# A two-block transformer layer in one kernel: the second expert stage regrouped by weight rows, with a class of 32 tokens in four column tiles

## The reference

```python
logits = (xt @ router_w + router_b).astype(jnp.float32)
top_v, top_e = lax.top_k(logits, TOP_K)            # 4 of 32
gate = jax.nn.softmax(top_v, axis=-1)
def expert_block(args):
    rows, e = args
    xb = xt[rows]
    hb = xb @ w1[e] + b1[e]                        # w1[e]: 1024 x 2048
    g, u = hb[:, :D_EXPERT], hb[:, D_EXPERT:]
    g = jnp.minimum(g, SWIGLU_LIMIT)
    u = jnp.clip(u, -SWIGLU_LIMIT, SWIGLU_LIMIT)
    glu = g * jax.nn.sigmoid(g * SWIGLU_ALPHA)
    return ((u + 1.0) * glu) @ w2[e] + b2[e]       # w2[e]: 1024 x 1024
```

## Time and profile before

| what | us |
| --- | --- |
| three timed runs, median | 2508.3 |
| lowest and highest of them | 2503.12, 2519.26 |
| the profiled execution | 2512.87 |
| its span in the trace | 2511.1 |
| second expert stage in it, first up product to last down product | 1145.33 |

### The profile page before, as it was taken

One profiled execution on the slowest core, in us unless ns is written; L12 is line 12 of the kernel. 1 busy time (PEld: TensorE's weight loads), 2 busy tenths in 40 slices (PEclk: granted clock), 3 DMA queues, 4 the chain that ended last, 5 costly groups with the idle time before them and its releaser, 6 DMA issues.

```text
span 2511.1 us, 32392 instructions
## 1 busy us (share of the span) xinstructions
PE 2247.6 (90%) x12228; PEld 1328.1 (53%) x12229; DVE 589.5 (23%) x1216; ACT 370.2 (15%) x718; POOL 6.5 (0%) x23
## 2 busy tenths in 40 slices
PE   7969877889998997788858999899999999999996
PEld 5655445556545686633335554445455555555553
DVE  2352512211222015500031212111221222222113
ACT  1032101121111014300011111101011111111111
POOL 1000000000000000000000000000000000000000
PEclk9989997999999976588877989999998999999998
DMA  8822253998966340022225999859799999999990
GB/s 289 317 101 82 86 201 120 327 356 312 325 224 233 102 150 19 1 100 100 100 78 198 393 363 345 312 202 380 270 386 381 339 393 376 393 383 393 384 370 18
DMA packets 272763, 621.67 MB, mean 248 GB/s; under 512 B 12200, under 2 KB 19026, under 8 KB 272510
## 3 DMA queue, kind: packets, MB, share of 16 engines
q1 hardware_dynamic: 272302, 616.95, 67.1%
q10 hardware_dynamic: 208, 0.67, 0.1%
HBM read 616.55 MB, written 1.05 MB: 246 GB/s over the span
## 4 chain that ended last, share of the span: by engine, by line
PE 87%; DVE 6%; issue 4%; ACT 3%; POOL 0%; ACTq 0%; DVEq 0%; POOLq 0%
PE pair L1616 26%; PE pair L1410 16%; PE pair L1652 10%; PE pair L1671 8%; PE pair L1397 6%; PE pair L1689 4%; PE pair L1621 3%; PE pair L1655 2%; PE pair L1459 2%; PE pair L1451 1%; PE pair L1825 1%; PE pair L1434 1%; PE pair L1422 1%; PE pair L1702 1%; PE pair L1414 1%
## 5 line engine op out<-in xcount | busy, mean ns | idle before, releaser
L1616 PE MATMUL pair<-ring,r_at 128*64 128x256 f32 (+1 forms) x4864 | 662.0, 402 | 53.2 <-issue 49.5
L1616 PEld LDWEIGHTS pair<-ring,r_at 128*64 128x64 f32 (+1 forms) x4864 | 385.6, 143 | 317.2 <-issue 177.2
L1652 PE MATMUL pair<-ring,r_big 128*64 128x512 f32 x1152 | 263.9, 609 | 0.0
L1410 PE MATMUL pair<-ring,x_T 128*128 128x512 f32 (+1 forms) x608 | 236.9, 545 | 2.5 <-ACT r_big L719 1.1
L1671 PE MATMUL pair<-r_big,r_mix 128*128 128x64 f32 (+1 forms) x1600 | 204.3, 290 | 23.1 <-DVE r_big L1338 11.4
L1671 PEld LDWEIGHTS pair<-r_big,r_mix 128*128 128x128 f32 x1600 | 197.8, 205 | 34.0 <-issue 33.2
L1173 DVE TENSOR_SCALAR r_big<-iota,rank 128x128 f32<-128x128 f32 x100 | 24.1, 283 | 752.0 <-PE pair L1621 577.0
L1410 PEld LDWEIGHTS pair<-ring,x_T 128*128 128x128 f32 x608 | 107.5, 190 | 125.0 <-issue 123.0
L1652 PEld LDWEIGHTS pair<-ring,r_big 128*64 128x64 f32 x1152 | 80.4, 140 | 151.2 <-issue 149.9
L1397 PE MATMUL pair<-x_T,ring 128*128 128x256 f32 x656 | 152.8, 391 | 7.8 <-DVEq L838 6.4
L1397 PEld LDWEIGHTS pair<-x_T,ring 128*128 128x128 f32 x656 | 125.9, 195 | 32.3 <-issue 8.0
(11 more groups left out here) (310 smaller groups left out, 1602.7 us busy)
## 6 DMA issues: line engine op xcount, KB each, us to landing
ring<-exp_w SPq DMA_DIRECT2D x192, 2048.0 KB, 12.5
ring<-w_in SPq DMA_DIRECT2D x24, 2048.0 KB, 9.2
ring<-w_gate SPq DMA_DIRECT2D x16, 2048.0 KB, 11.4
ring<-w_up SPq DMA_DIRECT2D x16, 2048.0 KB, 13.4
ring<-w_down SPq DMA_DIRECT2D x16, 2048.0 KB, 9.2
ring<-mod_w SPq DMA_DIRECT2D x12, 2048.0 KB, 13.5
ring<-w_out SPq DMA_DIRECT2D x4, 2048.0 KB, 8.0
ring<-w_branch SPq DMA_DIRECT2D x3, 2048.0 KB, 7.6
```

Source lines behind the costliest of these rows:

```text
L1410: ins = mm(out[:, t, 0:n], xT[:, k, P * t:P * t + P], w[:, k, c0:c0 + n], start=(k == 0), stop=(k == nk - 1 and bias is None))
L1616: ins = mm(out, stat(k), w_[:, k, c0:c0 + n], start=(k == 0), stop=(bias is None and k == KD - 1))
L1652: ins = mm(ps[2][H2 * h:H2 * h + H2, 0:512], hT[:, at:at + H2], cols, start=beg, stop=end)
```

## The change

- The loads of an expert are now four of 256 whole rows of w1 (8 KB each) and two of w2 as before. All four quarters of the hidden columns are built up side by side over the four loads (`up`), in `ps[0]` (and `ps[1]`).
- A fourth class: up to 32 tokens. There each product fills 32 columns of the array, and the four quarters of the columns go to four column tiles. In down, the four parts of the contraction go to the four tiles; they are summed by the scatter, for which the slots' numbers are repeated four times (`slots_of`). With 64 slots the same is done with two.
- Gather and scatter are always made for 128 slots (`gather2`, `scatter2`), with no choice by size; the class of all 256 tokens adds its outputs in `outputs_of_all` and scatters zeros.
- The hidden rows are formed once an expert and turned at once; the scatter stands after up, then the next gather, then turn and down.
- The size is chosen twice in an expert (`up` and `down`), with nested `If`/`Else` from the smallest.
- The first expert stage gets functions of its own (`gather1`, `scatter1` and so on) with the same work as before.
- Ahead of the stage, three copies write `slots_of`, and `ranks` has two more vector instructions for 32 experts.

The core of the diff:

```diff
+        def smallest_first(eng, size, body):
+
+            with eng.If(size == 0):
+                body(H4)
+            with eng.Else():
+                with eng.If(size == 1):
+                    body(H2)
+                with eng.Else():
+                    with eng.If(size == 2):
+                        body(P)
+                    with eng.Else():
+                        body(T)
...
-            def expert2(slot, kind, e, half, wait):
+            def expert2(slot, part, e, wait):
                 sp.wait_ge(PD, wait)
-                if kind < 2:
-                    src = w1e[bass.ds(e * D, D), 1024 * kind + 512 * half:1024 * kind + 512 * half + 512]
-                    nk = KD
+                if part < 4:
+                    src, nk = w1e[bass.ds(e * D + 2 * P * part, 2 * P), :], 2
                 else:
-                    src = w2e[bass.ds(e * D + 512 * half, 512), :]
-                    nk = 4
+                    src, nk = w2e[bass.ds(e * D + 512 * (part - 4), 512), :], 4
...
+            def hidden_T2(e, w):
+
+                act.wait_ge(sem("hidden_turned2"), e + 1)
+                n = min(8 * w, 1024)
+                ins = s.copy(HTF[:, 0:n], ps[0][:, 0:n])
+                if w == T:
+                    ins = s.copy(HTF[:, 1024:2048], ps[1])
+                ins.then_inc(sem("hiddenT_ready2"), 1)
...
+                n = 512 if b == 1 and w == H2 else 1024
+                if b == 1 or w != T:
+                    act.wait_ge(PD, pd_down)
+                    s.copy(YS[:, 0:n], ps[2][:, 0:n]).then_inc(sem(f"ys_ready{b}"), 1)
...
+            rows_of(2, 0)(P)
             with looped(act, 0, NE2) as e:
-                size, size_next = size_of(act, e), size_of(act, e + 1)
+                size = size_of(act, e)
 
                 def body(w):
-                    for half in range(2):
-                        act.wait_ge(sem("gate_limited"), 2 * e + (1 + half))
-                        if half:
-                            act.wait_ge(sem("hidden_ready2"), 2 * e + 1)
-                        s.activation(SG[:, 0:4 * w], GS[:, 0:4 * w], ACT.Sigmoid, scale=1.702)\
-                            .then_inc(sem("sig_ready"), 1)
-                    turned(2, 0, e, w)
-                    by_size(act, size_next, rows_of(2, e + 1))
-                    turned(2, 1, e, w)
+                    rows, n = (H2, 512) if w == H4 else (P, 512) if w == H2 else (P, 1024)
+                    if w == T:
+                        act.wait_ge(sem("up_times_gate"), e + 1)
+                        ins = s.activation(GSG, GSG, ACT.Sigmoid, scale=1.702)
+                    else:
+                        act.wait_ge(sem("gate_limited"), e + 1)
+                        ins = s.activation(SG[0:rows, 0:n], GS[0:rows, 0:n], ACT.Sigmoid, scale=1.702)
+                    ins.then_inc(sem("sig_ready"), 1)
+                    rows_of(2, e + 1)(P)
+                    hidden_T2(e, w)
                     outputs_and_picks(2, e, w, 6 * e + (base_pd2 + 6))
 
-                by_size(act, size, body)
+                smallest_first(act, size, body)
...
+                slots = iota if b == 1 else slots_of[:, bass.ds(size_of(dve, e) * P, P)]
                 for t in range(NT):
-                    ins = v.tensor_scalar(pick[:, buf, t], iota, rank[:, t, bass.ds(e, 1)], None, ALU.is_equal)
+                    ins = v.tensor_scalar(pick[:, buf, t], slots, rank[:, t, bass.ds(e, 1)], None, ALU.is_equal)
...
+            for c, w in enumerate((H4, H2)):
+                link(v.tensor_copy(slots_of[:, P * c:P * c + P].rearrange("p (q s) -> p q s", s=w),
+                                   iota[:, 0:w].unsqueeze(1).broadcast_to([P, P // w, w])))
+            link(v.tensor_copy(slots_of[:, 2 * P:4 * P].rearrange("p (q s) -> p q s", s=P),
+                               iota.unsqueeze(1).broadcast_to([P, 2, P])))
...
+            def hidden2(e, w):
+
+                dve.wait_ge(PD, 6 * e + (base_pd2 + 4))
+                if w == T:
+                    for t in range(NT):
+                        ins = v.tensor_scalar(GSG[:, 1024 * t:1024 * t + 1024], ps[2 * t], 7.0, None, ALU.min)
+                    ins.then_inc(sem("gate_limited"), 1)
+                    for t in range(NT):
+                        ins = v.tensor_scalar(HID[:, t], ps[2 * t + 1], 7.0, -7.0, ALU.min, ALU.max)
+                    gate, up, sig, out = GSG, HIDF, GSG, HIDF
+                else:
+                    rows, n = (H2, 512) if w == H4 else (P, 512) if w == H2 else (P, 1024)
+                    gate, up, sig, out = [x[0:rows, 0:n] for x in (GS, US, SG, HIDF)]
+                    g_in, u_in = {H4: (ps[0][0:H2, 0:512], ps[0][H2:P, 0:512]), H2: (ps[0][:, 0:512], ps[0][:, 512:1024]),
+                                  P: (ps[0], ps[1])}[w]
+                    v.tensor_scalar(gate, g_in, 7.0, None, ALU.min).then_inc(sem("gate_limited"), 1)
+                    ins = v.tensor_scalar(up, u_in, 7.0, -7.0, ALU.min, ALU.max)
+                ins.then_inc(up_free, 1)
+                dve.wait_ge(sem("gate_limited"), e + 1)
+                dve.wait_ge(up_free, e + 1)
+                v.scalar_tensor_tensor(out=up, in0=up, scalar=1.0, in1=gate, op0=ALU.add, op1=ALU.mult)\
+                    .then_inc(sem("up_times_gate"), 1)
+                dve.wait_ge(sem("up_times_gate"), e + 1)
+                dve.wait_ge(sem("sig_ready"), e + 1)
+                v.tensor_tensor(out=out, in0=up, in1=sig, op=ALU.mult).then_inc(sem("hidden_ready2"), 1)
+
+            def outputs_of_all(e):
+
+                dve.wait_ge(PD, 6 * e + (base_pd2 + 6))
+                for t in range(NT):
+                    for h in range(2):
+                        v.scalar_tensor_tensor(out=ACC[:, t, 512 * h:512 * h + 512], in0=ps[2 + t][:, 512 * h:512 * h + 512],
+                                               scalar=comb0[:, t, bass.ds(e + 1, 1)],
+                                               in1=ACC[:, t, 512 * h:512 * h + 512], op0=ALU.mult, op1=ALU.add)
+                v.memset(YS, 0.0).then_inc(sem("ys_ready2"), 1)
...
+                        hidden2(e, w)
+                        dve.wait_ge(sem("hidden_ready2"), e + 1)
                         add_outputs(2, e, ACC)
-                        hidden2(e, 1, w)
-
-                    by_size(dve, size_of(dve, e), body)
-                    dve.wait_ge(sem("hidden_ready2"), 2 * e + 2)
+                        if w == T:
+                            dve.wait_ge(sem("outputs_added2"), e + 2)
+                            outputs_of_all(e)
+
+                    smallest_first(dve, size_of(dve, e), body)
+                    dve.wait_ge(sem("outputs_added2"), e + 2)
+                    dve.wait_ge(sem("ys_ready2"), e + 2)
...
+            def up_parts(w):
+
+                x32, x64, x128 = [lambda k, n=n: XG[:, k, 0:n] for n in (H4, H2, P)]
+                if w == H4:
+                    return [(ps[0][H4 * q:H4 * q + H4, 0:512], x32, q, H4) for q in range(4)]
+                if w == H2:
+                    return [(ps[0][H2 * (q % 2):H2 * (q % 2) + H2, 512 * (q // 2):512 * (q // 2) + 512], x64, q, H2)
+                            for q in range(4)]
+                if w == P:
+                    return [(ps[q // 2][:, 512 * (q % 2):512 * (q % 2) + 512], x128, q, P) for q in range(4)]
+                return [(ps[2 * t + q // 2][:, 512 * (q % 2):512 * (q % 2) + 512],
+                         lambda k, t=t: XT[:, k, P * t:P * t + P], q, P) for t in range(NT) for q in range(4)]
+
+            def up(j, i, size, e, buf):
+
+                def body(w):
+                    if w >= P:
+                        pe.wait_ge(sem("pickT_ready2"), e + 1)
+                    if w == T:
+                        pe.wait_ge(sem("ys_ready2"), e + 1)
+                        pe.wait_ge(sem("outputs_added2"), e + 1)
+                    for n in range(4):
+                        pe.wait_ge(slot_loaded[(j + n) % RING], value_of(j + n, i, 6))
+                        w_ = ring[:, ((j + n) % RING) * SLOT:((j + n) % RING + 1) * SLOT]\
+                            .rearrange("p (t n) -> p t n", t=2)
+                        for k in range(2 * n, 2 * n + 2):
+                            for out, stat, q, rows in up_parts(w):
+                                ins = mm(out, stat(k), w_[:, k % 2, 512 * q:512 * q + 512], start=(k == 0), stop=False)
+                        if n == 3:
+                            for out, stat, q, rows in up_parts(w):
+                                ins = mm(out, ones[32 * q:32 * q + 1, 0:rows], b1q[32 * q:32 * q + 1, buf], start=False,
+                                         stop=True)
+                        ins.then_inc(PD, 1)
+                    if w >= P:
+                        pe.wait_ge(up_free, e + 1)
+
+                smallest_first(pe, size, body)
...
+            def down(j, i, size, e):
+
+                def body(w):
+                    if w == H4:
+                        for c in range(4):
```

(62 more changed lines are left out.)

190 lines of the change are left out of this document (75 added, 115 removed).

## The result

The changed kernel takes 2538.7 us (median of 4, 2527.3 to 2549.0) against 2505.7 us of the kernel before on the same chip (median of 4, 2501.2 to 2519.3): ratio 1.0121, interval 1.0062 to 1.0181. It is slower by 1.2%, where 2430 was forecast. The profiled execution is the 2527.3 us one.

What follows compares the result with a forecast made beforehand. TensorE and the loads were both taken as near their limits. With loads as pace, 939 + 4 + 47 + 34 + 36 = 1060 us of stage against 1145.3; 2512.9 - 85.3 + 2 = 2430 us, range 2395 to 2455 (0.48).

Steps and rivals of the forecast that it cites:

- I add 3 us for a lower clock (below) and jumps: 24: TensorE's small expert (at most 32 tokens): 20.9 us of work plus 3 us for clock and jumps, 24 us.
- about 1.5 for the jump over the smaller class's body: Experts of 33 to 64 tokens: TensorE's jump, covered by no queued work, takes about 1.5 us.
- debt: TensorE's lag behind the loads: each large expert inside the stage falls 31 us behind; a small one pays off 6 us.
- C: Rival: TensorE waiting for loads lowers its clock in small experts, 28 to 30 us each; 2480 to 2510 us; chance 0.11.
- Four column tiles: Small class's up and down: four tiles four times as fast as full width; up 6.9 us, bias 1.05, down 3.45.
- Rival A: Four column tiles run only two at a time: up 13.8 us, down 7; 2562 us, slower; chance 0.09.
- Rows of 8 KB: Loads of the first weight go at 419 GB/s, 5.0 us each against 5.45; an expert's six take 30.3 us.
- Rival B: The 8 KB rows bring nothing (385 GB/s): 32.1 us of loads an expert; 2465 us; chance 0.19.
- The new wait behind the turn: Small experts: TensorE stands about 1.2 us before down while ScalarE copies the gathered, then the turned rows.
- Large experts: Over 64 tokens (4 experts): 61 us each against 54, with new waits for picks (1.3 us) and PSUM (2.6 us).
- Class of 33 to 64: Six experts: column work of up and down as before, full scatter, jump added; 34 us each against 30.6.
- The sum: Second expert stage, loads as pace plus debts: 1060 us against 1145.3, giving 2430 us.

Runs made afterwards that it cites:

- e10: Changed kernel with TensorE's second expert stage held twice, without and with the 256-token class, chosen once ahead of the loop: 2431.8 us, ratio to before 0.9683.
- e11: Changed kernel with the 256-token body replaced by dead products, another number at each of the four places of a pass: 2481.0 us (one run).
- e7: e2 without the 32-token class, so that small experts go by the 64-token class: 2494.1 us, ratio 0.993.
- e12: e2 with w1 read in 2 KB pieces, two loads of 1 MB for a slot: 2466.3 us, ratio 0.9815.
- e2: Changed kernel without TensorE's 256-token code in up and down of the second stage: 2430.1 us, ratio 0.9669.
- e1: Changed kernel with the size chosen for each load (four up slots, the turn, each down half), so no jump exceeds 12.3 KB: 2507.0 us, ratio 0.9997.
- e6: e2 with the 256-token code for four experts put back as one never-taken branch at each pass's end: 2466.1 us, ratio 0.9811.
- e9: Changed kernel with the 256-token class kept as an expert of its own, chosen once at the expert's start: 2593.6 us, ratio 1.0325.

## Why the prediction was wrong

**The step that failed** is the jumps' part of "I add 3 us for a lower clock (below) and jumps: 24", with the "about 1.5 for the jump over the smaller class's body" beside it. Jumps were counted by how many there are ("two size choices an expert instead of some eleven"), as a thing of which fewer is better. The runs show that what counts is how much code a jump passes, with a step at some 20 KB: both jumps reach it here, none of the eleven did. A small expert pays 2.7 to 4.1 us behind bias and 1.5 to 2.8 us more in scatter, whose granted clock has fallen after the stand, and ten of the 22 pay another 1.8 to 3.5 us behind down. With short jumps (e10) a small expert that waits for nothing takes 20.8 us, as the sum before those 3 us had it (20.9); in the changed kernel one without a wait for loads, inside a pass, takes 28.4 to 31.6. That is the pace of the loads, and so the second half of the error: no small expert pays off anything of the debt a large one leaves, on which the sum's 1060 us rested.

No rival named it. C had a part of the consequence (the clock takes it back) with another cause, the wait for loads; over the changed kernel's stage the granted clock is 0.89, where C wanted under 0.75, and in e10, which waits for loads more, it is 0.92 and the gain stands. The prediction's own sign of being wrong (small experts more than 33 us apart or less than 28) missed it: they stand 31.6 us apart.
The Trainium skill (Runtime: NRT & Kernel Launch, Instruction fetch mechanics) has the mechanism: instructions are fetched ahead in sequence, in blocks of 16 KiB, and a taken branch out of a window of two blocks stops the engine until its target is fetched. The traces agree: packets of 16 KB, one landing in or just before each stand, no stand at 18.4 KB in most cases, one in every small expert at 37 KB. With two blocks a jump of between one and two block lengths is free or not by where in its block it starts. That fits the 20.0 KB behind down, which stand at two places of the pass and not at the other two; it doesn't explain the five values at 18.4 KB in e11, which all lie at the same place, so the moment matters too. Neither was tried by itself. The same section also gives TensorE 128 KiB; with a window of that size the jumps of 18 to 37 KB should have cost nothing, and the measurement decides against it.

**Four column tiles**: up x64 in 7.07 us (forecast 6.9), bias 0.99 (1.05), down 3.64 (3.45). Rival A falls. The tiles are worth 64 us (e7).

**Rows of 8 KB**: 417 to 425 GB/s (419). Rival B falls, and its price was right: 35 us forecast for no gain from the rows, 36 measured (e12 against e2).

**The new wait behind the turn**: 1.2 us forecast, 34.0 us in 28 waits measured (L1776 above), 1.2 each.

**Large experts**: 61, measured 61.2 and 58.7 in e10. The first is partly luck: the three take 63.9, 60.3 and 59.3 us, and the 63.9 hold one stand of 6.2 us behind the wait for PSUM, which ends 1.55 us after an instruction packet has landed. Of its terms, the wait for the up rows to leave PSUM is there as said (2.6 forecast), here the last expert of the changed kernel:

```profile
2473.49 1.23 DVE r_big L1380
2474.72 1.14 DVE r_big L1381
...
2476.38 5.37 PE pair L1837 x8
```

**Class of 33 to 64**: 34 forecast; 37.8 measured, 34.1 in e10. The jump over 27.6 KB behind up accounts for 1.3 us of the 3.7 (stands of 1.5 to 2.5 us in four of six); in two of the six up takes 20.5 us, not 16.7, one of them with a stand of 2.36 us inside it that ends 1.4 us after a packet has landed. The rest stays open.

**The sum**: with the long jumps gone (e10) the stage from first up product to last down product is 1058.6 us, where 1060 was forecast (1165.0 in the changed kernel), and the time 2431.8, where 2430 was. Most terms hold one by one, so this is not luck alone. That it comes out within 2 us is luck, since some of them cancel: the 3 us for clock and jumps aren't needed by a small expert that waits for nothing, a large one takes 58.7, not 61; small experts follow each other in 28.2 us in the mean, under the 30.3 of the loads, because behind a large one they run at TensorE's pace, and debts and waits at pass starts take more than their share (stands of up to 9.3 us ahead of up).

**Why e1 gained little** is settled only in part. Its packets (160) show that short jumps pass code that is fetched, and each of its experts has some 76 KB of it, five packets in 31.7 us for a small one. Stands inside up and behind bias say that in a burst of four slots TensorE outruns the fetch: 21 of the 26 stands over 1.5 us inside or ahead of up end 1.4 to 1.8 us after a packet has landed. The packets around the chain shown start at 1362.8, 1369.4, 1375.4, 1381.2 and 1387.6 us. Of the 159 distances over the stage 102 are 5.5 to 6.5 us and eight are shorter. Five of them take nearly as long as the whole expert, so the fetch may well be e1's pace. No run varies it alone, and after a long jump two packets come closer together (0.5 us in e6).

## What to carry to other kernels

Before putting a choice of bodies on an engine's path, count the code that the taken branch jumps over. Below some 18 KB it was mostly free here; from 20 to 28 KB it cost 1.5 to 4.1 us or nothing, by its place; at 37 KB it always cost, 2.7 to 4.1 us, plus what a fallen clock takes from the work behind it. A rare class costs even if it never runs. Put such a class where it is jumped over once (a second copy of the loop behind one choice), not where every turn of the loop meets it, and read a stand of cause "issue" between two helpers as a question to the program's layout: see whether an instruction packet lands just before the stand ends.

## What was not expected of the hardware

- Beyond the step the price grows little with the length: 21.5 KB behind bias cost 3.3 to 4.1 us, 37 KB 2.7 to 4.1. For 115 KB (e6) it is 36 us of time over eight jumps, with the wait at a pass start 7.3 us longer in the mean.
- The stands of the changed kernel end 1.4 to 1.8 us after a packet of 16 KB has landed, all 37 of them.
- TensorE can outrun the fetch inside a body too: 1.09 us inside up in e9, behind a long jump, and 3.80 us inside up in e1, behind short ones.
- The stand costs twice: after 3.94 us of nothing the granted clock over scatter was 0.61 and scatter took 5.95 us. In e10 scatter's mean is 690 ns a record against 841.
- Four column tiles of 32 columns run fully side by side in float32: 64 records in 7.07 us, where two tiles of 64 columns take 13.88 (e7).
